# Attention in a hybrid decoder step: four copies of gated values on ScalarE instead of GpSimd, and the order planner's weights set anew

## The reference, cut to what matters

```
u, a_gate, q, kv_c, kv_s, kv_w, g, b_gate = even_project(x, w_in)
a_out = silu(layer_norm(conv(u))) * silu(a_gate)         # the gated values: 512 channels
b_out = nsa_block(...)   # per 128 queries: three softmaxes (selected, window, compressed), times gates g
y = concat([a_out, b_out * silu(b_gate)]) @ w_out
```

## Time and profile before

| | |
|---|---|
| time, median of 3 runs | 1083.73 us (1083.7 to 1083.9) |
| the profiled execution's own time | 1075.91 us |
| its span, first to last instruction | 1074.1 us |
| busy: PE, DVE, ACT, POOL | 1024.5, 768.1, 369.7, 361.6 us |
| mean granted TensorE clock | 0.994 of full speed |
| attention phase | from about 378 to 658 us of the span |

### The profile page before, as it was taken

How to read it: one execution, slowest core, us unless ns; L and a number is a source line. 1 busy time by engine, 2 the same in 40 slices (tenths; PEclk the granted TensorE clock), 3 DMA queues, 4 the chain that set the end, 5 groups by cost and what they waited for, 6 DMA issues and landing times.

```text
span 1074.1 us, 19275 instructions
## 1 busy us (share of the span) xinstructions
PE 1024.5 (95%) x7750; PEld 874.1 (81%) x7750; DVE 768.1 (72%) x1406; ACT 369.7 (34%) x784; POOL 361.6 (34%) x373
## 2 busy tenths in 40 slices
PE   7898999999999989989899999999999999999997
PEld 7888999999999955656555666788999999997885
DVE  4677889999899978887577757786545710268955
ACT  4201111212222667878466756011112211344000
POOL 3443630000110397865685554100122311318000
PEclk9999999999999999999999999999999999999998
DMA  9644421153322034130673058342231121041321
GB/s 300 200 153 159 141 90 46 40 181 103 114 41 45 1 110 139 41 120 1 224 245 123 2 181 237 103 157 78 61 97 39 40 57 47 1 157 64 123 105 72
DMA packets 85666, 113.74 MB, mean 106 GB/s; under 512 B 21729, under 2 KB 66921, under 8 KB 85504
## 3 DMA queue, kind: packets, MB, share of 16 engines
q1 hardware_dynamic: 71849, 69.51, 21.3%
q0 software_dynamic: 11552, 41.95, 11.5%
q10 hardware_dynamic: 2182, 1.16, 0.4%
HBM read 100.90 MB, written 16.64 MB: 109 GB/s over the span
## 4 chain that ended last, share of the span: by engine, by line
PE 77%; DVE 11%; issue 4%; POOL 3%; DMA 3%; ACT 2%; another core or an unknown queue 1%; SPq 0%; DVEq 0%; POOLq 0%; ACTq 0%
PE PS L794 24%; PE PS L2223 16%; PE PS L1976 12%; PE PS L1309 5%; PE PS L1327 4%; PE PS L1439 4%; PE PS L776 3%; PE PS L2004 2%; DVE XL L2395 2%; DMA WRAW<-in_w_in_even 1%; DVE ACC L615 1%; PE PS L2203 1%; DVE PT L1497 1%; DVE GT L2390 1%; POOL PRW L1719 1%
## 5 line engine op out<-in xcount | busy, mean ns | idle before, releaser
L662 DVE SCALAR_TENSOR_TENSOR Y<-U,SM,Y 128x1024 f32<-128x1024 f32 x120 | 150.2, 1312 | 0.4
L794 PE MATMUL PS<-XH,WH 128*128 128x352 f32 x600 | 136.2, 331 | 0.0
L794 PE MATMUL PS<-XL,WH 128*128 128x352 f32 x600 | 133.5, 326 | 0.0
L794 PE MATMUL PS<-XH,WL 128*128 128x352 f32 x600 | 132.6, 325 | 0.0
L615 DVE SCALAR_TENSOR_TENSOR ACC<-PS,SM,ACC 128x508 f32<-128x508 f32 x124 | 86.9, 741 | 24.7 <-PE PS L776 21.3
L2328 POOL TENSOR_TENSOR WL<-WRAW,WH 128x1024 fp32r<-128x1024 f32 x14 | 37.4, 2674 | 195.8 <-ACT WH L2275 195.8
L794 PEld LDWEIGHTS PS<-XH,WH 128*128 128x128 f32 x600 | 101.0, 188 | 1.3
L794 PEld LDWEIGHTS PS<-XH,WL 128*128 128x128 f32 x600 | 101.5, 188 | 0.0
L794 PEld LDWEIGHTS PS<-XL,WH 128*128 128x128 f32 x600 | 101.2, 188 | 0.0
L1497 DVE COPY PT<-PS 128x512 f32<-128x512 f32 (+1 forms) x80 | 51.8, 647 | 35.8 <-PE PS L1309 21.0
L2223 PE MATMUL PS<-XH,WH 128*128 128x352 f32 x360 | 77.2, 323 | 0.0
(11 more groups left out here) (366 smaller groups left out, 1991.6 us busy)
## 6 DMA issues: line engine op xcount, KB each, us to landing
WRAW<-in_w_in_even SPq DMA_DIRECT2D x16, 512.0 KB
WRAW<-in_w_in_odd SPq DMA_DIRECT2D x16, 512.0 KB, 4.1
TM<-in_state_win_kv SPq DMA_DIRECT2D x12, 512.0 KB
XIN<-in_x_prompt SPq DMA_DIRECT2D x8, 512.0 KB, 7.4
WRAW<-in_w_in_even SPq DMA_DIRECT2D x16, 256.0 KB
XR<-in_x_prompt SPq DMA_DIRECT2D x8, 512.0 KB, 3.6
layer_out<-R SPq DMA_DIRECT2D x8, 512.0 KB, 2.6
XR<-layer_out SPq DMA_DIRECT2D x8, 512.0 KB, 3.3
```

The source lines that it names most:

```text
L662: v.scalar_tensor_tensor(dst, src, CWT[:, i, t:t + 1], dst, ALU.mult, ALU.add).then_inc(s_cv, 1)
L794: ins = pe.matmul(PS[0:mcols, 3 * slot + c, 0:CH], w[:, slot, kk, 0:mcols], x[:, kk, c * CH:(c + 1) * CH], start=(kk == 0 and n == 0), sto ...
```

## The change

The four casts move from POOL's list to ACT's. Their waits stay the same: D 11 (`s_mm`), and the gated slice (`s_yg` or `s_ya`); so do those who wait for them (`s_ah`). The planner gets them as a kind `("ACT", "A")` of 1110 instead of 1060 ns. All of the planner's weights are replaced: 17 entries by engine and kind instead of 12, and an entry for nearly every engine, kind and eighth instead of 14.

```diff
         for i in range(4):
-            step("POOL", "A", ("cast", i), 1060, (("D", 11), PE_END), (("gated", 3), 100))
+            step("ACT", "A", ("cast", i), 1110, (("D", 11), PE_END), (("gated", 3), 100))
             step("DVE", "H", ("H", i), 1570, (("cast", i), 100))
...
-        PREFER = {("ACT", "E"): -23000, ("ACT", "P"): 53000, ("ACT", "X"): -28000, ("DVE", "M"): -28000, ("DVE", "O"):
-                  -69000, ("DVE", "P"): 465000, ("DVE", "X"): -164000, ("PE", "D"): 118000, ("PE", "T"): 2000, ("PE", "V"):
-                  -114000, ("PE", "X"): -67000, ("POOL", "C"): 134000}
...
+        PREFER = {('ACT', 'E'): -38000, ('ACT', 'P'): 54000, ('ACT', 'X'): -74000, ('DVE', 'M'): -102000, ('DVE',
+                  'O'): -120000, ('DVE', 'P'): 252000, ('DVE', 'X'): -332000, ('PE', 'D'): 71000, ('PE', 'T'): 2000,
+                  ('PE', 'V'): -308000, ('PE', 'X'): -50000, ('POOL', 'C'): 407000, ('DVE', 'H'): 403000, ('POOL',
+                  'X'): -153000, ('DVE', 'R'): -35000, ('POOL', 'A'): 307000, ('ACT', 'A'): -34000, ('PE', 'S'):
+                  -1000}
...
@@ -1539,6 +1575,11 @@
                 elif ev[0] == "gate":
                     evac(NM)
+                elif ev[0] == "cast":
+                    i = ev[1]
+                    act.wait_ge(s_mm, NM + 1)
+                    act.wait_ge(*((s_yg, i + 1) if i < 2 else (s_ya, i - 1)))
+                    copy(XH[:, i, :], Y[:, i, :]).then_inc(s_ah, 1)
...
@@ -1743,14 +1784,6 @@
-                elif ev[0] == "cast":
-                    i = ev[1]
-                    po.wait_ge(s_mm, NM + 1)
-                    if i < 2:
-                        po.wait_ge(s_yg, i + 1)
-                    else:
-                        po.wait_ge(s_ya, i - 1)
-                    po.tensor_copy(XH[:, i, :], Y[:, i, :]).then_inc(s_ah, 1)
```

More of the change, by code:

```diff
@@ L1233, in program @@
         assert len(remains) == len(about)
-        PREFER = {("ACT", "E"): -23000, ("ACT", "P"): 53000, ("ACT", "X"): -28000, ("DVE", "M"): -28000, ("DVE", "O"):
-                  -69000, ("DVE", "P"): 465000, ("DVE", "X"): -164000, ("PE", "D"): 118000, ("PE", "T"): 2000, ("PE", "V"):
-                  -114000, ("PE", "X"): -67000, ("POOL", "C"): 134000}
[L1239 to L1242, removed]
+        PREFER = {('ACT', 'E'): -38000, ('ACT', 'P'): 54000, ('ACT', 'X'): -74000, ('DVE', 'M'): -102000, ('DVE',
[4 rows of a table added]
+        PREFER_EIGHTH = {('ACT', 'E', 2): -299000, ('ACT', 'E', 3): -118000, ('DVE', 'R', 1): 247000, ('PE', 'D', 0):
[37 rows of a table added]
         order = {e: [] for e in todo}
```

## The result

The changed kernel takes 1089.87 us (median of 7 runs, 1088.91 to 1091.86), the kernel before in the same comparison 1083.73 us (7 runs): ratio 1.0079, 95% interval 1.0060 to 1.0099. The forecast was 1079.6 us, faster, with a range up to 1085.5; the result lies outside it. The profiled execution took 1088.91 us, span 1087.1, against 1075.91 and 1074.1 before.

A forecast was written before the change was run, and what follows sets the result against it. PE was taken as the bound, busy 1024.5 of 1074.1 us, so only its idle time could be won. Hole -3.0, clock -1.1, rest 0 gave -4.1: 1083.7 to 1079.6 us, range 1075.0 to 1085.5.

The forecast's parts named there:

- the other 258 us: Attention phase after its first 22 us: ranks mostly unchanged, taken as 0, between -4 and +4 us.
- -3.0 at T 2: PE's idle hole at 388 to 400 us: T 2 begins at about 394.9 against 397.95; bounds 0 and -3.8 us.
- S 3 and S 4 ahead of D 11: Sign at the attention phase's start: these score steps precede the last held-back projection step in PE's timeline.
- E of pair 3 at 387: Sign at the attention phase's start: M and E of pair 3 were forecast before 388 us.
- predicted in the list 1.3 to 1.6: Sign on DVE: each low operand H takes 1.3 to 1.6 us once the casts leave POOL.
- no table load behind the casts: ACT's casts between gate and exponentials add no table load, taken as 0; bound one more load, 1.28 us.
- C 3 ended before 391: Sign on POOL: scaling C 3, which T 2 needs, ends before 391 us, against 396.09.
- -1.1 for the clock: PE's clock dip at 398 to 402 us goes with the hole: 1.1 us won; other bound 0.
- The port: DVE's H no longer slowed beside POOL's casts: 0 to 2.4 us of DVE's time back, 0 in the sum.
- Rival (b): Slower: ACT's casts hold up the copies, about +2.7 us, 1086.4, or a worse later order by over 2 us; chance 0.2.
- Rival (d): Moving the casts does nothing; the moved S alone close the hole, time as forecast; no separate chance given.
- Rival (a): The hole at the attention phase's start moves to the next T: only 0 to 1 us won; chance 0.22.

The follow-up runs named there:

- e1: The changed kernel with PE's last values step V 79 moved in front of Y 0 instead of behind Y 1; ratio to the kernel before 1.0009.
- e2: The kernel before with only V 79 moved behind Y 0 and Y 1 in PE's list; ratio to the kernel before 1.0061.
- e3: The kernel before with the casts on ACT and its old weights kept, replanned; ratio to the kernel before 1.0026.
- e6: e1 with the seven first-quarter gathers behind C 4 put one by one behind C 6 to C 12 on POOL; ratio to the kernel before 0.9980.
- e8: The kernel before with e5's casts on ACT, e7's move of H 2, and three first-quarter gathers behind C 6 to C 8; ratio 0.9998.
- e5: The kernel before, order and weights kept, with only the four casts put by hand into ACT's list; ratio to the kernel before 1.0004.
- e12: e6 with the four casts put back on POOL, two behind C 4 and two behind C 5; ratio to the kernel before 1.0030.
- e4: The kernel before with the new weights but the casts left on POOL, replanned; ratio to the kernel before 1.0091.
- e7: The kernel before with only DVE's low operand H 2 moved behind the copy of T 1; ratio to the kernel before 1.0014.
- e9: e6 with the copies of T 1 and T 2 moved ahead of H 1 and H 2 (DVE), the samples' exponential and casts 2, 3 (ACT); ratio 0.9995.
- e10: e6 with later rows of gathers taken apart, all but the first of a row put behind following steps; ratio to the kernel before 1.0120.
- e11: e6 with the edits of e9 and e10 together; ratio to the kernel before 1.0133.

## Why the prediction was wrong

**Where it failed most.** "I take 0", the term for the other 258 us, with a bound of +4 and the reason that "the ranks mostly do not" turn. I replayed the planner at the phase's start and not at its end, and compared only V's weight with those of its usual rivals. The end comes out of the planner's own times, in us from the start of its plan. New weights: PE ends V 78 at 258.75. Y 0 could begin at 258.84, V 79 at 259.24, since it waits for the copies of T 79. The 0.40 us between them are more than `NEAR`, so Y 0 goes first whatever V's weight is. Only against Y 1 (264.38 to 264.48) does the score decide, 5.5 to 1.6 - 308 - 41 = -347 thousand. Old weights: a samples' step, `("ot", 1)`, stands between V 78 and V 79 and fills that wait, V 79 begins at 255.93, and Y 0 is not ready before 256.95. The new weights had moved `("ot", 1)` ahead of T 78; the traces have it so (PE's 128x128 transpose at 656.39 in before, behind V 78, and at 658.37 in after, ahead of T 78). What the runs showed in place of the 0 is 7.6 us for this step (e1), 6.6 in reverse (e2). The bound was wrong in kind as well: it was made from the idle PE inside the phase, and the 7.6 us arose behind it.

**-3.0 at T 2** was +0.4 in after and -0.1 in e1. The replay of the order was right in the parts it gave: S 3 and S 4 ahead of D 11, E of pair 3 at 387, gate, casts 0 and 1, then the copy of T 0. The sizes were right: casts of 2.05 / 2 = 1.03 us (predicted 1.08), H of 2.42 / 2 = 1.21 (predicted in the list 1.3 to 1.6, in before 1.26 to 2.24), no table load behind the casts. What failed was to take T 0's recorded end as the time at which its copies can start, and to leave POOL's list out of the replay. With the casts gone, gathers are all that POOL has ready behind C 4 while it waits for C 5, so three stand in a row, whatever their weight; e3, with the casts moved and the old weights, has four in a row at 390.7. e6 shows that without the row T 2 is 2.65 us earlier than in e1 (7.25 - 4.60), and 2.8 earlier than in before. The price of the step was about right, and a consequence of the move that I had not looked for took it. The forecast wanted C 3 ended before 391; the four PRW scalings ended at 391.56, and it made no difference.

**-1.1 for the clock** was a loss: 6.8 us of half clock at 395 and 3.4 more at 405, where before had 3.4 there. It stands at the hole, and e6, with a shorter hole, has 3.4. The Trainium skill (TensorE: Matmul & The Clock Gate, "HAM oscillation") puts such falls behind idle gaps of PE; after's two longest ones since its first matmul, 4.08 us until 397.6 and 3.75 until 700.3, agree, each beside a stretch at 1.2 of 2.4 GHz (windows 388:400 and 699:706). A gap's length alone does not tell: after's falls at 405 and 467 stand behind 1.91 and 1.38 us of idle PE, and e8 was idle for 2.45 us until 398.5 and kept its full clock there.

**The port**, 0 in the sum with a bound of 2.4. What came back on DVE is near the bound: e6's four H take 2.42 + 2.46 = 4.9 us against 7.16 before. What it is worth in time depends on the order: nothing in e5, a part of the 3 to 5 us by which e12 is behind e6, where 0.8 us in the H pair and 0.9 in a two-column instruction are its own and the rest is not told apart from the places of the casts.

**The rivals.** Rival (b), slower, had 0.20, for casts that hold the copies, which after does not have, though e3 does. It also counted "an order in the later stages that is worse by over 2 us"; that half came true, by more and without a place named. Rival (d), that the move does nothing, is what e5 says of before's order, but the hole did not close by the moved S alone either (e4, 4.84 us of idle PE ahead of T 1). Rival (a) is e7. The start of the phase came out as a mixture of (a) and something I had not listed. Of e1's +2.1 us from T 0 to Y 0 against before, half a microsecond is there at T 3; the rest falls in the later stages and I did not find its place. T 0 itself comes 0.5 us later behind the last block's first matmul (19.3 us against 18.8), which D 0 to D 2 ahead of S 0 and the samples' step ahead of T 0 may explain; no run tells.

## What to carry to other kernels

When a planner's weights change, look at the last step of each kind against everything that becomes ready beside it, not at the kinds' usual ranks, and at the times as well as the scores: here a step of 1.2 us lost its turn to 11 us of other work because it was ready 0.4 us later, and the end of a phase is where a misplaced step has no cover. When work leaves an engine, look at what then stands next to each other in its list. Price a closed hole only after asking which queue is late next and what the clock does, since here 1.6 us won at T 2 (e7), or 2.7 at T 3 (e9), were all lost again within 20 us. Keep rows of POOL's indirect DMAs away from a place where other engines wait for PE, but not so far that their data comes late.

## What the runs showed of the hardware

**PE's results are seen late beside indirect DMAs.** After: 3.2 us with three gathers in a row; e1: 2.8 us with the same three; e6: 0.1 us with none. Later rows show the same: in the attention phase of the profiles of twelve of the fourteen kernels, two to five transposes each have copies with "remote" as releaser, all of them during or up to 1.2 us behind a row of two to four gathers. e10 and e11, with most rows taken apart, have none, and e10 cut the waits for DVE's copies from 15.2 to 8.8 us. Not every row has such a wait. Whether the transposes themselves or their signal are late is open: the Trainium skill (Perfetto Trace Analysis, "Tensor Engine Instruction (MATMUL, LD_WEIGHTS)") says that a matmul's end in a profile is an estimate and the signal comes after it; these records do not tell the two apart. Nor was a gather's issue told apart from its traffic.

**The start of the program varies, and with it every single profile.** Far from the change, at 29 to 31 us, the clock is at half for 0, 3.4 or 6.8 us. Windows 20 to 40 us of before, and then of e5:

```profile
20.00:40.00 20.00, 17.66 (x123) 16.55 (x124) 9.81 (x22) 6.41 (x12) 10.76 (x9) 1.00 0.78 267
```

```profile
20.00:40.00 20.00, 15.99 (x95) 15.20 (x96) 6.24 (x17) 4.79 (x11) 7.99 (x7) 0.83 0.77 265
```

T 0 lies at 390.6 in the one and 395.0 in the other. e2 and e7, whose programs are before's up to T 0, have it at 395.3 and 394.3. The kernel before took 1074.1 to 1084.8 us in 35 runs of one comparison. So the 7.8 us between its profiled execution and the median in front were no constant: that profile was near the fastest case. Eleven or twelve runs against 17 or more gave intervals of +-0.14 to 0.2%, so a difference of 0.2% is at the edge of what they tell.

**A short DVE instruction can wait for several of POOL's.** 2.90 us beside four casts of 1.02 us (e4), 1.08 beside two (e12), 0.17 without (after). In both it ended with POOL's last cast, at 398.70 against 398.66 and at 397.31 against 397.28.
